# A streaming encoder step on one core: products of zeros and a small Exp ahead of the data, gate weights ahead of natural x, the norm's factor in two steps, gate tiles ahead of keys

## The chip, the cores and the metric

One NeuronCore of a Trainium2 chip. The metric is the device time in microseconds of one execution, lower is better. A core has TensorE (PE in the profile, with its weight loads as PEld), VectorE (DVE), ScalarE (ACT), GpSimd (POOL) and SyncE (SP, which here issues all transfers). Each engine works through its own list of instructions in order and waits on semaphores for the others.

## What is computed

One inference step of a two-layer encoder over 512 prompt frames and 8 streams of 16 sample frames, 640 rows of 1024 in all: a gated linear attention layer (GLA), a shared latent key and value side, and an attention layer that reads it. The change lies in the first layer:

```python
def gla_layer(x, S0, norm_pre, w_in, w_gate2, b_gate, head_norm, w_out, norm_post):
    h = rmsnorm(x, norm_pre)
    proj = h @ w_in
    q, k, v, gate, glr = jnp.split(
        proj, [KD_A, 2 * KD_A, 2 * KD_A + VD_A, 2 * KD_A + 2 * VD_A], axis=-1)
    z = (glr @ w_gate2 + b_gate).astype(jnp.float32)
    g = jax.nn.log_sigmoid(z) / GATE_TAU
    ...
    o, S = gla_core(heads(q, DK_A) * (DK_A ** -0.5), heads(k, DK_A), heads(v, DV_A),
                    heads(g, DK_A), S0.astype(jnp.float32))
    o = rmsnorm(o.transpose(0, 2, 1, 3), head_norm.reshape(H_A, DV_A)).reshape(B, T, VD_A)
    o = o.astype(x.dtype) * jax.nn.silu(gate)
    return x + rmsnorm(o @ w_out, norm_post), S
```

`gla_core` walks over chunks: scores of q times exp(b) and k times exp(-b), with b the running sum of g, times v, plus the carried state.

## The kernel before

All work is a list of steps that `steps()` (L115) writes out by hand; every engine runs through the list in order and does its part of each step, as `PARTS` says. A step's parts follow one another by semaphores (`after`). So the order in the list is the order in each engine's queue. Matrices are kept as a rounded part and a rest (hi, lo), so a product is three products on PE (`mm3`, L1477 to L1479).

The rows are 5 tiles of 128 (4 of the prompt, 1 of the samples). The first layer has 4 heads. Its steps near the change, in the order of the list:

- `xk k`: ACT scales a slice of transposed x (hat_hi, L949), DVE makes the rest (hat_lo, L1212). `piece name j`: a block of weights, loaded by SP into one of 4 stage buffers (`load_stage`, L736; the next load into a buffer waits until DVE has read it), rounded by ACT (slab_hi, L922), its rest by DVE (slab_lo, L1175). `vx k`: PE's products of slice k with v of head 0 and the low-rank gate, 5 tiles of 272 columns, 3 products each, 8 slices: 120.
- `xn t`: ACT sums the squares of natural x, tile t (L953). `rq`: POOL makes the norm's factor r and the products of it that others use (rr and so on, L861 to L866).
- `gf`, `gfh`, `gfl`: the low-rank gate times r, by DVE, ACT, DVE. `vg i`: v of head 0 times rr, by ACT and DVE, out of the banks of `vx` (three steps for five tiles). `glT`: PE transposes the low-rank gate (L1533), ACT copies it. `gw`: its second weight.
- `g0 t`: the output gate of head 0, tile t: 24 products, tanh on ACT (L970), product on DVE (L1229).
- `z u`: PE, then DVE (z_abs, L1235) and ACT (Exp, then `ln`: Ln, which loads another activation table, L979), `lg` and `lgh` (DVE, ACT, DVE), and then `c h`: PE's running sums (L1557).
- `qp h` and `k h`: query and key of head h, 48 products of 320 columns each; `em`, `e`, `q`, `qlo`, `klo`: the exponentials and their products. `kT`, `sc`, `U`, `os`, `Us`, `o`: transposed keys, scores, state update, and outputs of samples and prompt.

PSUM has 8 banks. Up to `c 3` they are given out by hand (`FIRST_BANKS`), then in a ring; a step on PE waits until the last reader of its banks is done (`before_bank`). `q_own`, `minus_half` and `gl3` are set by POOL before all else (L841 to L845).

Before, PE's order around the change is: vx 0 to 7, g0 0, glT, g0 1, z, qp 0, g0 2, c 0, k 0, c 1, kT 0, c 2, c 3, sc 0, U 0, g0 3, g0 4, os 0, Us 0, o 0, qp 1, k 1, v 1. SP's order is x and the first weights in turn, natural x (5 tiles), the two gate pieces of head 0, gate3, const, the gains, and then loads as buffers come free.

Of the kernel before, what the change touches and what calls it, by code (L numbers as in the profile page):

```python
# [28 lines left out]
VG = DV + RANK  # L29
Z_ORDER = (0, HA, 2, 3, 1)  # L30
# [84 lines left out]
def steps():  # L115
# [6 lines left out]
    for k in range(KD):  # L122
        out += [("xk", k)]
        if k % 2 == 0:
            out += [("piece", "v0g", k // 2)]
        out += [("vx", k)]
    out += [("xn", t) for t in range(NT)]
    out += [("rq",), ("const",), ("piece", ("g", 0), 0), ("gf",), ("piece", ("g", 0), 1), ("gfh",), ("gfl",), ("vg", 0), ("gw",)]
    out += [("g0", 0), ("glT",), ("vg", 1), ("vg", 2), ("piece", ("qk", 0), 0), ("g0", 1)]
    out += [("z", u) for u in Z_ORDER] + [("qp", 0), ("piece", ("qk", 0), 1)]  # L130
    out += [("ln", 0), ("lg", 0), ("ln", HA), ("lg", HA), ("ln", 2), ("lg", 2), ("lgh", 0), ("lgh", HA), ("ln", 3), ("lg", 3), ("ln", 1), ("lg", 1)]
    out += [("g0", 2), ("c", 0), ("em",), ("e", 0), ("lgh", 1), ("q", 0), ("lgh", 2), ("lgh", 3), ("qlo", 0), ("k", 0), ("klo", 0)]
    out += [("c", 1), ("kT", 0), ("c", 2), ("c", 3)]
    out += [("lds", 0)]
    for h in range(HA):
        last = h + 1 == HA
        if h:
            out += [("e", h), ("qp", h), ("q", h), ("k", h), ("qlo", h), ("klo", h)]
# [3 lines left out]
        if not h:  # L142
            out += [("vo",), ("U", h), ("g0", 3), ("sclo", h), ("g0", 4), ("Slo", h), ("stp", h)]
            out += [("piece", ("qk", 1), 0)]
# [10 lines left out]
        else:  # L155
            if not h:
                out += [("piece", ("qk", 1), 1), ("o", h)]
                load(("v", h + 1))
            else:
                load(("v", h + 1))  # L160
                out += [("o", h)]
            out += [("lds", h + 1)]
# [90 lines left out]
def samples(out, load):  # L253
# [26 lines left out]
    "och": ("sp",), "y0": ("pe", "act", "dve"), "oy": ("sp",), "keep": ("sp",), "ldk": ("sp",), "yt": ("pe", "act", "dve"), "sum": ("pool",), "xk": ("act", "dve"), "xn": ("act",), "vx": ("pe",), "rq": ("pool",), "gw": ("act", "dve"),  # L280
# [16 lines left out]
def parts(step):  # L297

    if step == ("c", 0):
        return ("pe",)  # L300
    if step[0] == "piece" and not any(w[5] for w in SLABS[step[1]][step[2]]):
        return ("sp", "act", "dve")
# [13 lines left out]
STAGED_NO = {s: n for n, s in enumerate(STAGED)}  # L316
FIRST_WEIGHTS = [STAGED_NO["piece", ("g", 0), j] for j in range(2)]
# [29 lines left out]
def read_out(step):  # L347

    if step[0] in ("qp", "z"):
# [10 lines left out]
FIRST_BANKS = {("vg", 0): (0, 1), ("vg", 1): (2, 3), ("vg", 2): (4,), ("g0", 0): (5,), ("glT",): (6, 7), ("g0", 1): (0,),  # L360
# [1468 lines left out]
```

## Time and profile before

| | us |
|---|---|
| three runs | 660.23, 659.3, 653.32 |
| median | 659.3 |
| the profiled execution | 654.99 |
| its span | 653.2 |
| PE busy in the span | 619.9 (95%) |
| DVE busy | 401.2 (61%) |
| ACT busy | 297.5 (46%) |
| mean granted TensorE clock | 0.991 |

PE is the engine that is busy nearly all the time; the others have room on average. Rows of the trace are read from the start of the span: the first number is the start in us, the second the length, and in brackets stands how long the engine sat idle before it and what ended that. A row with x5 groups five instructions in a row. TensorE's granted clock is given as a share of its full 2.4 GHz.

### The profile page before, as it was taken

The numbers are of one execution on the slowest core, as the hardware profiler recorded it, in microseconds if no ns is written. First come the engines' busy times: TensorE is split into PE (matmuls) and PEld (weight loads), VectorE is DVE, ScalarE is ACT, GpSimd is POOL, SyncE is SP. The second block draws the span as 40 slices with busy tenths as digits, with TensorE's granted clock in tenths as the row PEclk, the third lists the DMA queues.
The fourth block names the chain that finished last, engine by engine and source line by source line (L and its number), as shares of the span: only waits on it lengthen the run. The fifth ranks groups of instructions, "written<-read, shape, count | busy, mean of one in ns | idle before, by whom it ended". The sixth has DMA issues, their size and how long they took to land.

```text
span 653.2 us, 12063 instructions
## 1 busy us (share of the span) xinstructions
PE 619.9 (95%) x4702; PEld 598.4 (92%) x4702; DVE 401.2 (61%) x612; ACT 297.5 (46%) x578; POOL 123.7 (19%) x140
## 2 busy tenths in 40 slices
PE   5999999999999899997999999999999979989996
PEld 5989999999999799997999999988999978789996
DVE  5475755564564792258657767467788776664414
ACT  7785623432532352246323422365556667753311
POOL 0200200100030152236325400210000126630002
PEclk9999999999999899999999999999999999989999
DMA  8932280261262263232243410331111126766004
GB/s 317 332 108 65 64 259 18 66 204 55 74 193 66 73 228 112 83 112 98 67 113 84 129 65 2 112 85 30 34 29 38 49 81 199 236 214 255 1 1 162
DMA packets 66280, 73.68 MB, mean 113 GB/s; under 512 B 8112, under 2 KB 58544, under 8 KB 66096
## 3 DMA queue, kind: packets, MB, share of 16 engines
q1 hardware_dynamic: 66224, 72.91, 35.5%
q8 instruction: 38, 0.62, 0.4%
q14 instruction: 18, 0.15, 0.1%
HBM read 62.12 MB, written 10.78 MB: 112 GB/s over the span
## 4 chain that ended last, share of the span: by engine, by line
PE 64%; DVE 15%; ACT 11%; issue 4%; POOL 3%; DMA 3%; DVEq 0%; ACTq 0%; POOLq 0%
PE bank L1477 21%; PE bank L1479 20%; PE bank L1478 20%; DVE slab_lo L1175 2%; ACT prob L1109 2%; ACT slab_hi L922 2%; DVE pT_lo L1175 2%; DMA stage<-in_cache_ckv_dram 1%; DVE rows L1393 1%; DVE prob L1445 1%; DMA stage<-in_b_w_out_dram 1%; DVE qN_lo L1175 1%; DVE hat_lo L1175 1%; POOL skL L902 1%; POOL cn_lo L898 1%
## 5 line engine op out<-in xcount | busy, mean ns | idle before, releaser
L1477 PE MATMUL bank<-slab_hi,hat_hi 128*128 128x256 f32 (+2 forms) x600 | 171.8, 286 | 11.8 <-DVE slab_lo L1175 8.3
L1478 PE MATMUL bank<-slab_lo,hat_hi 128*128 128x256 f32 (+2 forms) x600 | 170.6, 284 | 0.0
L1479 PE MATMUL bank<-slab_hi,hat_lo 128*128 128x256 f32 (+2 forms) x600 | 170.5, 284 | 0.0
L1477 PEld LDWEIGHTS bank<-slab_hi,hat_hi 128*128 128x128 f32 x600 | 115.9, 193 | 12.7 <-DVE slab_lo L1175 8.5
L1478 PEld LDWEIGHTS bank<-slab_lo,hat_hi 128*128 128x128 f32 x600 | 116.0, 193 | 0.0
L1479 PEld LDWEIGHTS bank<-slab_hi,hat_lo 128*128 128x128 f32 x600 | 116.0, 193 | 0.0
L1175 DVE TENSOR_TENSOR slab_lo<-stage,slab_hi 128x1024 fp32r<-128x1024 f32 (+3 forms) x70 | 84.3, 1205 | 18.0 <-ACT slab_hi L922 16.0
L1477 PE MATMUL bank<-hat_hi,slab_hi 128*128 128x320 f32 x256 | 80.6, 315 | 0.6 <-DVE rows L1401 0.4
L1478 PE MATMUL bank<-hat_lo,slab_hi 128*128 128x320 f32 x256 | 79.8, 312 | 0.0
L1479 PE MATMUL bank<-hat_hi,slab_lo 128*128 128x320 f32 x256 | 79.7, 311 | 0.0
L922 ACT ACTIVATE slab_hi<-stage 128x1024 fp32r<-128x1024 f32 (+3 forms) x70 | 71.0, 1014 | 14.2 <-POOL stage L857 6.0
L1477 PEld LDWEIGHTS bank<-hat_hi,slab_hi 128*128 128x128 f32 x256 | 48.6, 190 | 1.4 <-DVE rows L1401 1.0
L1479 PEld LDWEIGHTS bank<-hat_hi,slab_lo 128*128 128x128 f32 x256 | 48.7, 190 | 0.0
L1478 PEld LDWEIGHTS bank<-hat_lo,slab_hi 128*128 128x128 f32 x256 | 48.7, 190 | 0.0
L1479 PE MATMUL bank<-slab_hi,oT_lo 128*128 128x256 f32 x160 | 45.4, 284 | 0.0
L1477 PE MATMUL bank<-slab_hi,qS 128*128 128x256 f32 x128 | 36.7, 287 | 0.0
L1478 PE MATMUL bank<-slab_lo,qS 128*128 128x256 f32 x128 | 36.3, 284 | 0.0
L876 POOL TENSOR_TENSOR stat<-stat,stat 128x1 f32<-128x1 f32 (+1 forms) x8 | 2.5, 311 | 169.6 <-ACT junk L1049 155.3
L1053 ACT ACTIVATE junk<-bank 128x256 bf16<-128x256 f32 x26 | 9.7, 384 | 51.1 <-PE bank L1479 51.1
L902 POOL TENSOR_TENSOR skL<-stage,skS 128x512 fp32r<-128x512 f32 x8 | 13.8, 1730 | 94.0 <-ACT skS L922 94.0
L1479 PEld LDWEIGHTS bank<-slab_hi,oT_lo 128*128 128x128 f32 x160 | 30.8, 193 | 0.0
L1171 DVE TENSOR_TENSOR y_rows<-bank,post 128x256 f32<-128x256 f32 (+1 forms) x14 | 7.5, 539 | 30.1 <-ACT junk L1053 19.6
(334 smaller groups left out, 1440.5 us busy)
## 6 DMA issues: line engine op xcount, KB each, us to landing
stage<-in_a_w_in_dram SPq DMA_DIRECT2D x22, 512.0 KB, 5.1
stage<-in_b_w_in_dram SPq DMA_DIRECT2D x10, 512.0 KB, 4.2
st_s<-in_state_gla_dram SPq DMA_DIRECT2D x4, 1024.0 KB, 7.0
out_dram<-st_s SPq DMA_DIRECT2D x4, 1024.0 KB, 5.3
stage<-in_a_w_out_dram SPq DMA_DIRECT2D x8, 512.0 KB, 4.6
stage<-in_ckvT_dram SPq DMA_DIRECT2D x8, 512.0 KB, 3.5
stage<-in_cache_ckv_dram SPq DMA_DIRECT2D x8, 512.0 KB, 4.1
stage<-in_b_w_out_dram SPq DMA_DIRECT2D x8, 512.0 KB, 3.9
```

What stands on the lines that cost most here:

```text
L898: last = pool.tensor_tensor(cn_lo[b][:, :, :], staged_as(kind, step), raw(cn_hi[b][:, :, :]), SUB)
L902: last = pool.tensor_tensor(skL[b][:, :], staged_as(kind, step), raw(skS[b][:, :]), SUB)
L922: return act.activation(out, in_, ACT.Copy)
L1053: last = act.activation(junk[:, i * 256:(i + 1) * 256], row[:, i * 256:(i + 1) * 256], ACT.Square, accum_out=S1(("y", ph, t), t=s))
L1109: last = act.activation(prob[u][:, c0:c0 + i + 1, :], bank[:, j, 0:(i + 1) * P].rearrange("p (s n) -> p s n", n=P), ACT.Exp, bias=S1(("S", ...
L1171: return dve.tensor_tensor(out, a, b, op)
L1175: return dve.tensor_tensor(lo, full, raw(hi), SUB)
L1393: last = dve.tensor_scalar(qln[:, t, :], qln[:, t, :], S1(("qa",), stat2, t), None, MUL)
L1445: last = dve.tensor_scalar(v, v, r[:, j:j + 1], None, MUL)
L1477: pe.matmul(out, a[0], b[0], start=first, stop=False)
L1478: pe.matmul(out, a[0], b[1], start=False, stop=False)
L1479: return pe.matmul(out, a[1], b[0], start=False, stop=last)
```

## The change

Six times PE multiplies q_own, all zeros, by itself as soon as it is set, ahead of everything else, into a bank that is written anew later; ACT takes an Exp of 8 columns of it. SP issues the two gate pieces of head 0 ahead of natural x, and const ahead of gate3; ACT and DVE take these pieces ahead of `xn`. `rq` ends with r; what is made from it is a step of its own, `rr`, and `vg` waits for that. On PE the order becomes: vx 0 to 7, g0 0, g0 1, glT, g0 2, z, qp 0, g0 3, c 0, g0 4, k 0, c 1, kT 0, c 2, c 3, sc 0, U 0, qp 1, os 0, Us 0, o 0, k 1, v 1, with other banks for it. The rest of the second piece of `qk 0` is taken from its step and becomes `plo`, behind the z products. The pieces of `qk 1` come earlier, and `qp 1` is copied by ACT into a part of the gate rows that is not yet in use, from where DVE takes it. The first weights of v 1 are taken ahead of `o 0`.

```diff
@@ -27,6 +27,7 @@
 VG = DV + RANK
+WARM = 6
 Z_ORDER = (0, HA, 2, 3, 1)
...
@@ -124,24 +125,24 @@
         out += [("vx", k)]
+    load(("g", 0))
     out += [("xn", t) for t in range(NT)]
-    out += [("rq",), ("const",), ("piece", ("g", 0), 0), ("gf",), ("piece", ("g", 0), 1), ("gfh",), ("gfl",), ("vg", 0), ("gw",)]
-    out += [("g0", 0), ("glT",), ("vg", 1), ("vg", 2), ("piece", ("qk", 0), 0), ("g0", 1)]
-    out += [("z", u) for u in Z_ORDER] + [("qp", 0), ("piece", ("qk", 0), 1)]
+    out += [("rq",), ("rr",), ("const",), ("gf",), ("gfh",), ("gfl",), ("vg", 0), ("g0", 0), ("gw",), ("g0", 1), ("glT",)]
+    out += [("vg", 1), ("vg", 2), ("piece", ("qk", 0), 0), ("g0", 2), ("piece", ("qk", 0), 1)]
+    out += [("z", u) for u in Z_ORDER] + [("qp", 0), ("plo", ("qk", 0), 1)]
...
-    out += [("g0", 2), ("c", 0), ("em",), ("e", 0), ("lgh", 1), ("q", 0), ("lgh", 2), ("lgh", 3), ("qlo", 0), ("k", 0), ("klo", 0)]
+    out += [("g0", 3), ("c", 0), ("em",), ("e", 0), ("lgh", 1), ("q", 0), ("g0", 4), ("lgh", 2), ("lgh", 3), ("qlo", 0), ("piece", ("qk", 1), 0), ("k", 0), ("klo", 0)]
     out += [("c", 1), ("kT", 0), ("c", 2), ("c", 3)]
...
         if h:
-            out += [("e", h), ("qp", h), ("q", h), ("k", h), ("qlo", h), ("klo", h)]
+            out += [("e", h)] + [("qp", h)] * (h > 1) + [("q", h), ("k", h), ("qlo", h), ("klo", h)]
             load(("g", h))
...
         if not h:
-            out += [("vo",), ("U", h), ("g0", 3), ("sclo", h), ("g0", 4), ("Slo", h), ("stp", h)]
-            out += [("piece", ("qk", 1), 0)]
+            out += [("vo",), ("U", h), ("qp", 1), ("sclo", h), ("Slo", h), ("stp", h), ("piece", ("qk", 1), 1)]
         else:
...
@@ -153,13 +154,8 @@
         else:
-            if not h:
-                out += [("piece", ("qk", 1), 1), ("o", h)]
-                load(("v", h + 1))
-            else:
-                load(("v", h + 1))
-                out += [("o", h)]
-            out += [("lds", h + 1)]
+            load(("v", h + 1))
+            out += [("o", h), ("lds", h + 1)]
     project_out(out, load, "A")
...
@@ -277,7 +273,7 @@
...
@@ -298,6 +294,10 @@
         return ("pe",)
+    if step == ("qp", 1):
+        return ("pe", "act")
+    if step == APART:
+        return ("sp", "act")
     if step[0] == "piece" and not any(w[5] for w in SLABS[step[1]][step[2]]):
...
@@ -314,6 +314,14 @@
 STAGED_NO = {s: n for n, s in enumerate(STAGED)}
+APART = "piece", ("qk", 0), 1
+
+
+def low_step(step):
+
+    return ("plo", *step[1:]) if step == APART else step
+
+
 FIRST_WEIGHTS = [STAGED_NO["piece", ("g", 0), j] for j in range(2)]
...
@@ -346,6 +354,8 @@
+    if step == ("qp", 1):
+        return "act", *step
     if step[0] in ("qp", "z"):
...
@@ -357,9 +367,9 @@
-FIRST_BANKS = {("vg", 0): (0, 1), ("vg", 1): (2, 3), ("vg", 2): (4,), ("g0", 0): (5,), ("glT",): (6, 7), ("g0", 1): (0,),
-               ("z", 0): (6,), ("z", HA): (7,), ("z", 1): (1,), ("z", 2): (2,), ("z", 3): (3,), ("qp", 0): (4, 5), ("g0", 2): (0,),
-               ("c", 0): (6, 7), ("k", 0): (2, 3), ("c", 1): (0, 1), ("kT", 0): (2, 3), ("c", 2): (6, 7), ("c", 3): (4, 5)}
+FIRST_BANKS = {("vg", 0): (0, 1), ("vg", 1): (2, 3), ("vg", 2): (4,), ("g0", 0): (5,), ("g0", 1): (6,), ("glT",): (0, 1), ("g0", 2): (7,),
+               ("z", 0): (0,), ("z", HA): (1,), ("z", 2): (2,), ("z", 3): (3,), ("z", 1): (6,), ("qp", 0): (4, 5), ("g0", 3): (7,),
+               ("c", 0): (0, 1), ("g0", 4): (6,), ("k", 0): (2, 3), ("c", 1): (6, 7), ("kT", 0): (2, 3), ("c", 2): (0, 1), ("c", 3): (4, 5)}
...
@@ -621,6 +631,8 @@
+        next_raw = rows[:, 3, D - TOK:D]
+
         def first_gate(t):
...
@@ -712,7 +724,7 @@
                     old = STAGED[n - NSTAGE]
-                    after(sp, parts(old)[-1], *old)
+                    after(sp, parts(old)[-1] if old != APART else "dve", *low_step(old))
                 if step[0] != "piece":
...
@@ -745,13 +757,13 @@
                     load_stage(k // 2)
+            for n in FIRST_WEIGHTS:
+                load_stage(n)
             for t in range(NT):
...
                              else dram["x_sample"].rearrange("b l d -> (b l) d")).then_inc(x_nat_in[t], 16)
-            for n in FIRST_WEIGHTS:
-                load_stage(n)
+            sp.dma_start(const[:, :], dram["const"]).then_inc(consts_in, 16)
             sp.dma_start(gate_raw[:, :], dram["gate3"]).then_inc(gate_in, 16)
-            sp.dma_start(const[:, :], dram["const"]).then_inc(consts_in, 16)
             for n, g in gain.items():
...
@@ -857,11 +869,13 @@
                     pool.wait_ge(done["act"], AT["act"][("xn", NT - 1)])
+                    r = S1(("r",), stat2)
+                    link(pool.tensor_scalar(r, S1(("x",)), 1.0 / D, EPS, MUL, ADD))
+                    last = pool.tensor_tensor(r, r, minus_half[:, 0:NT], ALU.pow)
+                elif kind == "rr":
                     r, rr = S1(("r",), stat2), S1(("rr",), stat2)
-                    link(pool.tensor_scalar(r, S1(("x",)), 1.0 / D, EPS, MUL, ADD))
-                    link(pool.tensor_tensor(r, r, minus_half[:, 0:NT], ALU.pow))
+                    link(pool.tensor_tensor(rr, r, r, MUL))
                     pool.tensor_scalar(S1(("rh",), stat2), r, 0.5, None, MUL)
-                    link(pool.tensor_tensor(rr, r, r, MUL))
                     pool.tensor_scalar(S1(("rrm",), stat2), rr, 1.0 / DV, None, MUL)
...
@@ -921,6 +935,8 @@
+            act.wait_ge(own_set, 1)
+            act.activation(junk[:, 0:8], q_own[:, 0, 0:8], ACT.Exp)
             act.wait_ge(first_gain_in, 16)
...
@@ -962,7 +978,7 @@
                 elif kind == "vg":
-                    act.wait_ge(done["pool"], AT["pool"][("rq",)])
+                    act.wait_ge(done["pool"], AT["pool"][("rr",)])
                     for t in range(2 * step[1], min(2 * step[1] + 2, NT)):
...
@@ -1007,6 +1023,8 @@
...
+                elif kind == "qp":
+                    last = copy(next_raw.rearrange("p (a n) -> p a n", a=2), bank[:, :, 0:HALF])
                 elif kind == "q":
...
@@ -1201,12 +1219,13 @@
                 bank, row = banks(step) if step in BANK_NO else (None, None)
-                if kind == "piece":
+                if kind in ("piece", "plo"):
                     _, name, j = step
+                    after(dve, "act", "piece", name, j)
                     m = used(name, j)
...
                     c = slice(j * PITCH[name], j * PITCH[name] + m)
-                    last = low(lo[:, c], stage[STAGED_NO[step] % NSTAGE][:, 0:m], hi[:, c])
+                    last = low(lo[:, c], stage[STAGED_NO["piece", name, j] % NSTAGE][:, 0:m], hi[:, c])
                 elif kind == "xk":
...
@@ -1247,8 +1266,12 @@
                         dve.wait_ge(own_set, 1)
-                    after(dve, "pe", "qp", h)
-                    v = banks(("qp", h))[0][:, :, 0:HALF]
+                    if h == 1:
+                        after(dve, "act", "qp", h)
+                        v = next_raw.rearrange("p (a n) -> p a n", a=2)
+                    else:
+                        after(dve, "pe", "qp", h)
+                        v = banks(("qp", h))[0][:, :, 0:HALF]
...
...
@@ -1506,6 +1529,9 @@
+            pe.wait_ge(own_set, 1)
+            for _i in range(WARM):
+                pe.matmul(pb[2][:, 1, 0:2 * P], q_own[:, 0:SB // 2, :], q_own[:, :, :].rearrange("p b n -> p (b n)"), start=True, stop=True)
             for step in STEPS:
...
@@ -1558,7 +1584,7 @@
                     h = step[1]
-                    after(pe, "dve", "piece", ("qk", h), 0 if kind == "qp" else 1)
+                    after(pe, "dve", *low_step(("piece", ("qk", h), 0 if kind == "qp" else 1)))
                     off = 0 if kind == "qp" else PIECE
...
                     for a in range(2):

```

## Rows read from the trace of the kernel before

**Rows 1.** The page's busy times and instructions by engine, whole span:
```profile
PE 619.9 (95%) x4702; PEld 598.4 (92%) x4702; DVE 401.2 (61%) x612; ACT 297.5 (46%) x578; POOL 123.7 (19%) x140
```

**Rows 2.** PE's waits, whole span: us in total, times, longest:
```profile
PE bank L1477 <- DVE slab_lo L1175: 8.3, 2, 7.9
...
PE bank L1557 <- DVE lg_lo L1175: 1.5, 1, 1.5
...
PE bank L1477 <- ACT decay L985: 0.4, 1, 0.4
```

**Rows 3.** Table by stretches: length, busy us (instructions), PEclk, DMA share, GB/s:
```profile
7.90:13.02 5.12, 5.12 (x23) 5.12 (x24) 4.93 (x6) 4.93 (x7) 0.00 (x0) 1.00 1.02 399
13.02:20.50 7.48, 7.48 (x61) 7.48 (x61) 3.41 (x5) 6.61 (x11) 0.00 (x0) 1.00 1.03 404
...
47.15:50.57 3.42, 3.42 (x16) 3.42 (x16) 0.73 (x3) 2.93 (x9) 0.00 (x0) 0.52 0.00 0
```

**Rows 4.** Timeline of PE in `k 0`: start, us, instruction:
```profile
47.34 0.47 PE L1478 MATMUL bank<-hat_lo,slab_hi 128*128 128x320 f32 x1
...
50.53 0.40 PE L1478 MATMUL bank<-hat_lo,slab_hi 128*128 128x320 f32 x1
...
55.60 0.31 PE L1479 MATMUL bank<-hat_hi,slab_lo 128*128 128x320 f32 x1
```

**Rows 5.** Timeline of ACT, start of the span:
```profile
3.86 1.28 ACT L949 ACT_TABLE_LOAD   x1 [3.86 <-DMA x_raw<-in_xT_dram]
...
6.02 0.66 ACT L922 ACTIVATE slab_hi<-stage 128x544 fp32r<-128x544 f32 x1
...
6.94 1.77 ACT L949 ACTIVATE hat_hi<-x_raw,gain_a_norm_pre 128x640 fp32r<-128x640 f32 x2 [0.26 <-DMA x_raw<-in_xT_dram]
```

**Rows 6.** Timeline of PE, the fp32 products of `os 0`:
```profile
69.43 1.07 PE L1614 MATMUL bank<-st_s,q_own 128*32 128x256 f32 x16
```

**Rows 7.** Timeline of ACT, POOL and DVE, the norm's factor:
```profile
20.50 1.06 ACT L953 ACTIVATE junk<-x_nat 128x1024 bf16<-128x1024 f32 x1 [0.19 <-DMA x_nat<-in_x_sample_dram]
...
23.51 1.06 ACT L922 ACTIVATE slab_hi<-stage 128x1024 fp32r<-128x1024 f32 x1 [0.45 <-DMA stage<-in_a_w_in_dram]
...
21.74 0.20 POOL L861 TENSOR_SCALAR stat<-stat 128x5 f32<-128x5 f32 x1 [19.78 <-ACT junk L953]
...
23.29 1.20 POOL L863 TENSOR_SCALAR stat<-stat 128x5 f32<-128x5 f32 x1
...
24.95 0.23 POOL L866 TENSOR_SCALAR stat<-stat 128x5 f32<-128x5 f32 x1
...
25.67 0.37 DVE L1171 TENSOR_TENSOR glf<-bank,stat 128x32 f32<-128x32 f32 x3 [1.28 <-PE bank L1479]
```

**Rows 8.** Timeline of ACT, DVE and PE, first v tiles and glT:
```profile
26.52 0.84 ACT L967 ACTIVATE vv_hi<-bank,stat 128x256 fp32r<-128x256 f32 x2
...
27.61 0.88 DVE L1226 SCALAR_TENSOR_TENSOR vv_lo<-bank,stat,vv_hi 128x256 fp32r<-128x256 f32 x2
...
28.88 0.71 PE L1533 MATMUL bank<-const,gl 128*128 128x128 f32 x5
```

**Rows 9.** Timeline of DVE, ACT and PE, from z to `c 0`:
```profile
34.68 3.59 DVE L1235 TENSOR_SCALAR z_abs<-bank 128x512 int32<-128x512 int32 x5
...
39.03 1.06 ACT L922 ACTIVATE slab_hi<-stage 128x1024 fp32r<-128x1024 f32 x1
...
40.11 1.28 ACT L979 ACT_TABLE_LOAD   x1
...
45.99 0.30 PE L1557 MATMUL bank<-const_r,lg_hi 128*128 128x130 f32 x1 [1.51 <-DVE lg_lo L1175]
```

**Rows 10.** Timeline of SP's DMA issues, DVE and POOL:
```profile
7.61 2.26 SPq L749 DMA_DIRECT2D x_nat<-in_x_prompt_dram  x4
...
9.73 0.72 DVE L1175 TENSOR_TENSOR slab_lo<-stage,slab_hi 128x544 fp32r<-128x544 f32 x1
...
31.53 2.48 POOL L869 TENSOR_SCALAR const_r<-const_raw 128x900 fp32r<-128x900 f32 x1 [6.35 <-DMA const_raw<-in_const_r_dram]
```

More of the change, by code:

```diff
@@ L279 @@
     "const": ("sp", "pool"), "piece": ("sp", "pool", "act", "dve"), "lds": ("sp",), "sts": ("sp",), "stp": ("sp",), "ldr": ("sp",),
-    "och": ("sp",), "y0": ("pe", "act", "dve"), "oy": ("sp",), "keep": ("sp",), "ldk": ("sp",), "yt": ("pe", "act", "dve"), "sum": ("pool",), "xk": ("act", "dve"), "xn": ("act",), "vx": ("pe",), "rq": ("pool",), "gw": ("act", "dve"),
+    "och": ("sp",), "y0": ("pe", "act", "dve"), "oy": ("sp",), "keep": ("sp",), "ldk": ("sp",), "yt": ("pe", "act", "dve"), "sum": ("pool",), "xk": ("act", "dve"), "xn": ("act",), "vx": ("pe",), "rq": ("pool",), "rr": ("pool",), "plo": ("dve",), "gw": ("act", "dve"),
     "gf": ("dve",), "gfh": ("act",), "vo": ("act",), "gfl": ("dve",), "vg": ("act", "dve"), "glT": ("pe", "act"), "g0": ("pe", "act", "dve"), "em": ("act",), "xT": ("pe", "act", "dve"),
```

## The prediction

> **What bounds the kernel now.** The page first: the products (PE) are busy 95% of the span [rows 1], so a change of order gains only where PE waits or runs slowly. The list of PE's waits, read next, shows three in the stretch that the diff touches: 8.3 us for slab_lo (7.9 of them before the first product, 0.4 more before the second half of the first gate tile), 1.5 for lg_lo, 0.4 for decay [rows 2]. The table by stretches shows what the waits leave out: between 7.90 and 13.02 us 23 products took 5.12 us (0.223 each), then 61 took 7.48 (0.123 each) [rows 3]. Same shape, twice the pace. The row's granted clock says 1.00 in both, so the record begins too late; 272 columns in 0.223 us is the 1.2 GHz level. At 47.15 to 50.57 the row itself says 0.52. It follows the 1.5 us wait. In `k 0` (48 products, the first at 47.13) the second starts at 47.34 and the fourteenth at 50.53, 0.266 apart; from there to the last the pace is (55.60-50.53)/34 = 0.149 [rows 4]. Lost: 12 x 0.117 = 1.4 us. So PE loses before 62 us: the late start, 23 x 0.100 = 2.3 slow, 0.4, 1.5, 1.4, 0.4. Behind 75 us the diff moves little, and a lead of PE there should reach the end.
>
> **Start: products of zeros, small Exp, and what they meet.** The table load runs 3.86 to 5.14, after x has landed; the first hat_hi follows it [rows 5]. The early Exp needs only a memset, so the load lies ahead of the data. The gain is not all of 1.28: the first slab_hi at 6.02 follows hat_hi at once, so the trace does not show when its weights had landed. Bounds 0 and 1.28; I take 0.6, the middle. The next hat_hi, 6.94, waits for DMA already, so no more than that is to be had.
>
> No row before shows full-width fp32 products. The nearest: 8 fp32 products of 32 by 256 columns (16 records) in 1.07 us [rows 6]. If four ran side by side, a full-width one costs 0.53; if not, 0.13. Six cost 0.8 to 3.2 us at full clock, twice that at half: they start near 1.2 and end between 2.8 and 7.6. Real work starts near 7.3, so they cost 0 to 0.3. Whether they raise the clock: before, it rose 5.1 us after the first product; six at the upper price are busy as long. I take it as up by about 7.3, the other bound being no effect. Then the 120 `vx` products take 120 x 0.123 = 14.8 and end at 22.1; without effect at 24.4. By the same rates they ended at 24.9 before (7.9 + 2.3 + 14.8).
>
> **The norm's factor decides what this is worth.** The gate weights (2 transfers) now go ahead of natural x (5). The seven move the same bytes, and the last of the seven was awaited by ACT until 23.51 before; the last x tile until 20.50 [rows 7]. So its square moves from 20.50 to about 23.4. From there, by rows of before: POOL starts 1.24 later (24.65), r is there 1.55 later (21.74 to 23.29: 26.2). `rr` must do the other four operations: they took 23.29 to 25.18, 1.9 us, of which one tensor_scalar is 1.20 while its like at 24.95 took 0.23. Bounds 0.9 and 1.9: rr at 27.1 to 28.1. `gf` and `gfl` no longer wait for rr (that is the split's gain, 0.9 to 1.9 on that branch). But the diff gives `glT` the banks (0, 1), which `vg 0` held, and these are free only when ACT and DVE have read v, for which they need rr: 0.84 + 0.88 and two handovers [rows 8], some 1.9. So `glT` can start at 29.0 to 30.0.
>
> PE gets there sooner: 22.1, then `g0 0` and `g0 1`, 24 products each (2.9), 27.9. It waits 1.1 to 2.1 us. Most of what the warm start gains is spent here; with no warm start it would arrive at 30.2 and hardly wait.
>
> The position "two gate tiles and glT done": before, 28.88 + 0.5 for the transposes (0.71 with their tail) + 2.9 = 32.3. After, 29.5 to 30.5. Ahead by 1.8 to 2.8.
>
> **Gate tiles ahead of keys.** `g0 2` moves ahead of the z products, `z` and `qp 0` are as before. Before, PE ran dry 1.51 us ahead of 45.99, at 44.48 [rows 9]; with the lead it gets there at 41.7 to 42.7, and `g0 3` (2.9) fills to 44.6 to 45.6. When are c 0's inputs ready? From glT's start DVE needed 5.8 us until its first z_abs (28.88 to 34.68); one more gate row is added and the row of g0 1 comes earlier, so I keep 5.8: 34.8 to 35.8. From z_abs to c 0 took 11.3; the weight piece's slab_hi (39.03, 1.06) leaves ACT's chain, and its slab_lo (`plo`) runs while ACT is still at Exp and the table load: 10.25. So c 0 at 45.05 to 46.05, beside 45.99 before, but with a fourth gate tile done. Ahead: 2.9 - 0.06 to 2.9 + 0.94, that is 2.8 to 3.8. What is late next is still this chain, by about half a microsecond.
>
> Two smaller moves on SP: const goes ahead of gate3 in the same group of transfers, and the load of const_r now stands behind two loads that wait for the gate pieces' slab_lo. POOL had const_r at 31.53 [rows 10] and c 0 needs it at 45; 3 or 4 us later costs nothing.
>
> With no long wait there, the slow stretch in `k 0` should go: 1.4. `g0 4` stands between c 0 and k 0 and only moves from later. Then c 1 takes banks (6, 7), so the scores no longer wait for ACT to empty c 2: 0.4. `qp 1` moves ahead of `os 0` and takes the place of g0 3 and 4; it is copied out by ACT (640 elements, so under the 1.06 of a piece with 1024 [rows 9]). Queued behind this copy on ACT are the second `qk 1` piece and the squares of os; for these POOL, then DVE wait, and `k 1` behind them. `qp 1` no longer lies between os and k 1, so 48 x 0.149 = 7.2 us less cover; what is left are Us and `o 0`, and behind them `k 1` (7.2) and `v 1` (96 products, 11.8) for the state update on DVE. I cost this at nothing; if the cover fails, it is the copy and the piece, up to 2.1.
>
> **The sum.** 2.8 to 3.8, plus 1.4, plus 0.4: 4.6 to 5.6, middle 5.1. The profiled execution took 655.0 us (span 653.2 and 1.8 around it): 649.9. But the three runs are 653.3, 659.3 and 660.2; the median is 4.3 above the profiled one. I know no reason for the changed kernel to fall on the quick side, so I take the middle of 655.0 and 659.3, 657.1, and predict 652.0.
>
> **Rivals.**
> 1. *The factor comes in time* (0.14). x lands sooner or POOL and the v tiles are quicker, and glT does not hold PE: 1.1 to 2.1 more, gain near 7, 650. For: rr's price rests on one odd row. Against: seven transfers came back to back, and ACT waited for them.
> 2. *The clock falls in the new wait* (0.24). The wait at glT is 1.1 to 2.1 us, and a wait of 1.5 came ahead of the slow stretch before [rows 2, 3]. Price 1.4, perhaps again in z and the c 0 chain: gain 3.0 to 3.7, 654. Against: the products on both sides of it are dense, while before c 0's small ones followed. The Trainium skill (TensorE: Matmul & The Clock Gate, section HAM oscillation — how this bites in real kernels) says that gaps between bursts of products bring the clock down again and that each burst then starts slow; by it the new gap speaks against this change. The trace agrees in that the slow stretch stands behind a wait; by the rule the sum is 651.3 on the profiled execution.
> 3. *Nothing net* (0.08). The z chain starts 3 us later than I put it (more queued on DVE between v and the gate rows), c 0 with it, and its wait is back with the slow stretch: 657.
> 4. *Slower* (0.04). SP issues natural x behind the second gate piece, and that waits for DVE to have emptied the second stage buffer, 10.45 before (9.73 + 0.72) [rows 10]. If the transfers ahead ran dry meanwhile, x would be late, and each microsecond goes one for one into the factor, glT, z and c 0. It decides from 5 us on (x at 28.5); over 1% slower needs 12, 668. Against: x used to be issued from 7.61 on, and what was queued by then kept the queue full far beyond 10.45.
>
> **How the numbers follow.** The forecast has 0.50. About 1% (6.6 us) is what a measurement of this kernel can tell from no change. Against the median of 659.3 the forecast is 7.3 below, so it counts as faster about as often as two times in three (0.33 to 0.17 same); rival 1 is faster (0.12 of 0.14), rival 2 less often (0.07 of 0.24); what is left of these and rival 3 are same (0.17 + 0.02 + 0.17 + 0.08 = 0.44, of which 0.01 goes to slower for the spread of the runs); rival 4 is slower. Faster 0.52, same 0.43, slower 0.05. Range: from rival 1 at the quick runs (653.3 - 7 = 646) to rival 3's 657 and a little: 646 to 657.5.
>
> **What would show it.** The first vx product before 7.9 and a pace of 0.123 there at once (or 0.223: no effect). The last x tile's square at 23 to 24 and the glT transposes at 29 to 30, behind a wait of PE for DVE's v tiles. No wait over 1 us ahead of c 0, no 1.2 GHz stretch in k 0, scores without their wait on decay. k 1 over some 5 us sooner than before. A second slow stretch at 28 to 34 says rival 2; glT near 28 without a wait says rival 1; a slab_lo or st_s wait ahead of k 1 or v 1 would be a cost I put at nothing.

## The result and the profile after

| | before | changed |
|---|---|---|
| median (18 runs of each) | 655.07 us | 650.69 us |
| lowest to highest | 651.35 to 660.3 | 647.64 to 654.42 |
| ratio, 95% interval | | 0.9945 [0.9924, 0.9965] |
| profiled execution (its span) | 654.99 (653.2) | 652.62 (650.8) |
| mean granted clock in it | 0.991 | 0.988 |

The changed kernel is 4.4 us faster between the medians. The ratio puts the gain at 0.55% (0.35 to 0.76%, or 2.3 to 5.0 us): clear of zero, but less than the 1% that the prediction called faster.

Busy times of the page of the changed kernel, the first number being PE's, and PE's waits up to 105 us (us in total, times, longest). They answer to [rows 1, 2].

```profile
PE 623.5 (96%) x4714; PEld 600.6 (92%) x4714; DVE 401.2 (62%) x612; ACT 298.4 (46%) x580; POOL 123.8 (19%) x140
...
PE bank L1559 <- DVE vv_lo L1245: 2.3, 1, 2.3
PE bank L1500 <- DVE slab_lo L1193: 1.5, 2, 1.3
PE bank L1534 <- POOL q_own L853: 1.1, 1, 1.1
PE bank L1601 <- DVE kt L1189: 0.8, 1, 0.8
```

PE is busy for 3.6 us more than before [rows 1]; the products of zeros add 4.4. Of the 8.3 for slab_lo 1.5 is left, beside 1.1 ahead of the zeros; the 1.5 for lg_lo and the 0.4 for decay [rows 2] are gone; a wait of 2.3 for the v tiles (vv_lo) and one of 0.8 for kt are new.

PE's timeline of the changed kernel: the zeros, the first vx products, glT with the gate tile behind it, z, c 0, the first and last of k 0, kT 0, kT 1.

```profile
1.08 4.41 PE L1534 MATMUL bank<-q_own 128*128 128x256 f32 x12 [1.08 <-POOL q_own L853]
6.81 0.36 PE L1500 MATMUL bank<-slab_hi,hat_hi 128*128 128x272 f32 x1 [1.32 <-DVE slab_lo L1193]
7.01 0.29 PE L1501 MATMUL bank<-slab_lo,hat_hi 128*128 128x272 f32 x1
7.14 0.29 PE L1502 MATMUL bank<-slab_hi,hat_lo 128*128 128x272 f32 x1
...
30.53 0.76 PE L1559 MATMUL bank<-const,gl 128*128 128x128 f32 x5 [2.28 <-DVE vv_lo L1245]
31.05 0.36 PE L1500 MATMUL bank<-slab_hi,hat_hi 128*128 128x256 f32 x1
35.50 0.56 PE L1569 MATMUL bank<-gate,glT 128*128 128x128 f32 x4
...
47.43 0.22 PE L1583 MATMUL bank<-const_r,lg_hi 128*128 128x130 f32 x1
...
51.42 0.31 PE L1500 MATMUL bank<-hat_hi,slab_hi 128*128 128x320 f32 x1
58.31 0.31 PE L1502 MATMUL bank<-hat_hi,slab_lo 128*128 128x320 f32 x1
...
60.47 0.74 PE L1601 MATMUL bank<-const,kt 128*128 128x128 f32 x5 [0.78 <-DVE kt L1189]
...
97.43 0.71 PE L1601 MATMUL bank<-const,kt 128*128 128x128 f32 x5
```

The second vx pair is 0.13 apart at once, where before 23 products took 0.223 each [rows 3]. The last row is kT 1, the first step behind v 1; up to there both kernels have done the same real products in another order. Before, it stood here:

```profile
100.49 0.71 PE L1575 MATMUL bank<-const,kt 128*128 128x128 f32 x5
```

So the lead is 3.1 us in these two executions. From kT 1 to the end of the span it is 552.7 before and 553.4 after.

Table by stretches of the changed kernel: length, PE busy and its instructions, the other engines, then PEclk, DMA share, GB/s.

```profile
6.81:22.30 15.49, 15.30 (x120) 15.12 (x121) 10.82 (x12) 12.22 (x17) 0.00 (x0) 1.00 1.03 384
...
31.60:35.00 3.40, 3.40 (x18) 3.40 (x17) 2.13 (x6) 2.87 (x5) 0.06 (x1) 0.50 0.42 140
...
51.42:58.31 6.89, 6.89 (x49) 6.89 (x48) 4.51 (x9) 3.96 (x6) 0.00 (x0) 1.00 0.00 0
```

All 120 vx products run at the full clock; k 0 has no slow stretch any more (0.147 a product throughout, against [rows 3, 4]). A slow one, at 1.2 GHz, stands behind the new wait instead: gate tile 2 takes 35.50 - 31.05 = 4.45 us where 24 products at full clock take 2.9.

The norm's factor in the changed kernel, from the timelines of ACT, POOL and DVE (answering to [rows 5, 7, 8]):

```profile
0.72 1.28 ACT L939 ACT_TABLE_LOAD   x1 [0.72 <-PEq L1827]
...
5.16 0.66 ACT L936 ACTIVATE slab_hi<-stage 128x544 fp32r<-128x544 f32 x1 [0.46 <-DMA stage<-in_v0g_dram]
...
24.85 1.06 ACT L969 ACTIVATE junk<-x_nat 128x1024 bf16<-128x1024 f32 x1 [0.15 <-DMA x_nat<-in_x_sample_dram]
...
28.66 0.84 ACT L983 ACTIVATE vv_hi<-bank,stat 128x256 fp32r<-128x256 f32 x2 [0.20 <-POOL stat L880]
...
26.09 0.20 POOL L873 TENSOR_SCALAR stat<-stat 128x5 f32<-128x5 f32 x1 [24.12 <-ACT junk L969]
26.37 1.18 POOL L874 TENSOR_TENSOR stat<-stat,minus_half 128x5 f32<-128x5 f32 x1
27.63 0.20 POOL L877 TENSOR_TENSOR stat<-stat 128x5 f32<-128x5 f32 x1
27.92 0.25 POOL L878 TENSOR_SCALAR stat<-stat 128x5 f32<-128x5 f32 x1
...
27.64 0.37 DVE L1189 TENSOR_TENSOR glf<-bank,stat 128x32 f32<-128x32 f32 x3 [7.47 <-POOL stat L874]
28.56 0.24 DVE L1193 TENSOR_TENSOR gl<-glf,gl 128x80 fp32r<-128x80 f32 x1 [0.55 <-ACT gl L936]
29.60 0.88 DVE L1245 SCALAR_TENSOR_TENSOR vv_lo<-bank,stat,vv_hi 128x256 fp32r<-128x256 f32 x2 [0.79 <-ACT vv_hi L983]
```

One chain ends in glT's wait: the last x tile lands, its square starts at 24.85, r is ready at 27.6, rr at 28.6, ACT makes v's rounded part, DVE its rest until 30.48, and glT starts at 30.53. Its own operand, the low-rank gate gl, is done at 28.80: the last 1.7 us of the wait are for banks 0 and 1, which hold v's first tiles until then and which the change gave to glT. No run gives it other banks, so what that would bring is open.

### The profile page after: what moved, and what is told of

Its sections match the earlier page's. It is cut to its first block, busy times and chain, and to the rows that moved or that the text cites. A ratio compares the mean times of both kernels' runs of the same rounds, so it can differ in the third digit from the quotient of the medians.

```text
span 650.8 us, 12087 instructions
## 1 busy us (share of the span) xinstructions
PE 623.5 (96%) x4714; PEld 600.6 (92%) x4714; DVE 401.2 (62%) x612; ACT 298.4 (46%) x580; POOL 123.8 (19%) x140
## 4 chain that ended last, share of the span: by engine, by line
PE 62%; DVE 16%; ACT 10%; DMA 4%; issue 4%; POOL 3%; SPq 1%; DVEq 0%; ACTq 0%; POOLq 0%
PE bank L1500 20%; PE bank L1502 19%; PE bank L1501 19%; DVE slab_lo L1193 2%; ACT prob L1127 2%; DMA x_nat<-in_x_sample_dram 2%; DVE pT_lo L1193 2%; DMA stage<-in_cache_ckv_dram 2%; ACT slab_hi L936 1%; DVE rows L1189 1%; DVE rows L1416 1%; DMA stage<-in_v0g_dram 1%; DVE prob L1468 1%; DVE qN_lo L1193 1%; POOL skL L916 1%
## 5 line engine op out<-in xcount | busy, mean ns | idle before, releaser
L1127 ACT ACTIVATE prob<-bank,stat 128x512 f32<-128x512 f32 (+3 forms) x32 | 16.6, 524 | 19.6 <-DVE stat L1458 19.4
```

What stands on the lines that cost most here:

```text
L1127: last = act.activation(prob[u][:, c0:c0 + i + 1, :], bank[:, j, 0:(i + 1) * P].rearrange("p (s n) -> p s n", n=P), ACT.Exp, bias=S1(("S", ...
```

## The experiments

Theory T: the norm's factor, held by the landing of natural x, sets when v's tiles leave their banks and so when glT starts; all that brings PE to glT sooner becomes waiting there, and from glT on the order with gate tiles ahead of keys keeps PE fed. A part of T, written into the expectations, was that the zeros even cost time, as the longer wait lets the clock fall. Rivals are named with each run. "kT 1" is the place in PE's timeline just used: 100.49 before, 97.43 in the changed kernel. Times are medians in us; the kernel before had 654.1 to 655.3 beside them.

**Without the zeros, and without zeros and Exp.**

```diff
-WARM = 6
+WARM = 0
```

> The changed kernel without its six products of zeros (the early Exp stays). Theory T: the products of glT wait for v's tiles and so for the norm's factor, at about 30.5 us, whenever PE gets there; the lead of the warm start is spent in that wait (2.3 us), and the clock falls behind it. Without the zeros vx runs at the 1.2 GHz level for some 5 us, ends near 24.6 instead of 22.3, the second gate tile near 30.4, glT starts at 30.5 after a wait under 0.4, no 1.2 GHz stretch follows, and kT 1 (97.4 in the changed kernel, 100.5 before) starts at 96.0. Time 1 to 2 us under the changed kernel's 650.7. Rival R: the warm start is what the change gains; without it all is 2.3 us later: kT 1 at 99.7, time 653.

648.15 in 4 runs, ratio 0.9891 [0.9857, 0.9926]. glT of this kernel, and the stretch behind it:

```profile
30.49 0.76 PE L1559 MATMUL bank<-const,gl 128*128 128x128 f32 x5 [0.19 <-DVE vv_lo L1245]
```

```profile
31.60:35.00 3.40, 3.40 (x31) 3.36 (x30) 2.12 (x6) 3.27 (x6) 0.13 (x1) 1.00 0.36 125
```

vx ends 2.0 later (24.3), and glT starts at the same place, 30.5, with next to no wait: what the zeros gain is waited away in full. kT 1 is at 96.41.

In the second kernel the small Exp on ACT is left out as well:

```diff
-            act.wait_ge(own_set, 1)
-            act.activation(junk[:, 0:8], q_own[:, 0, 0:8], ACT.Exp)
```

> The changed kernel without the zeros and without the early Exp. T: the first weights are rounded at 6.0 instead of 5.2, so 0.9 more than without the zeros alone; the second gate tile ends near 31.2, glT follows without a wait, no 1.2 GHz stretch behind it, kT 1 near 96.7. R: 3.2 us later than the changed kernel: kT 1 at 100.6.

651.55 (one run); kT 1 at 96.75.

```profile
30.27 0.71 PE L1557 MATMUL bank<-const,gl 128*128 128x128 f32 x5
```

With neither zeros nor Exp the new order alone has 100.49 - 96.75 = 3.7 us of the lead. The Exp adds 0.3, but not at glT: it starts here without a wait, and in the three profiles with the Exp and no zeros at 29.95, 30.49 and 30.50. The 0.3 arises behind glT: DVE's slab_lo at 34.38 took 1.86 us, as POOL's const_r had started 0.16 ahead of it, and 1.23 in the run without zeros, where it started first. So no part of the new start is seen to make glT earlier.

**The start alone, in the order of before.** The Exp and six products of zeros put into the kernel before, nothing else:

```diff
+            act.wait_ge(own_set, 1)
+            act.activation(junk[:, 0:8], q_own[:, 0, 0:8], ACT.Exp)
...
+            pe.wait_ge(own_set, 1)
+            for _i in range(6):
+                pe.matmul(pb[2][:, 1, 0:2 * P], q_own[:, 0:SB // 2, :], ...)
```

> The kernel before with only the new start: the early Exp and the six products of zeros. T: vx starts at 6.8 and ends at 22.3 (25.2 before), but the first gate weights are still rounded by 24.4 and 25.9, so g0 0 waits about 2 us and glT comes at 28.4 instead of 28.9; all later waits stay, so kT 1 is 0.5 sooner than the 100.5 of before, and if the clock falls in the new wait ahead of g0 0 it is about 1 later. Time within 1 us of the kernel before. R (the warm start is the gain): 3 us sooner, kT 1 at 97.5.

658.72 in 10 runs, ratio 1.0049 [1.0006, 1.0093]: no gain, rather a loss; kT 1 at 100.83. PE's waits in this kernel show where the early start went, and the stretch has its clock:

```profile
25.18 0.38 PE L1479 MATMUL bank<-slab_hi,hat_hi 128*128 128x256 f32 x1 [2.54 <-DVE slab_lo L1177]
27.68 0.39 PE L1479 MATMUL bank<-slab_hi,hat_hi 128*128 128x256 f32 x1 [0.81 <-DVE slab_lo L1177]
```

```profile
25.20:28.00 2.80, 1.99 (x14) 1.78 (x15) 1.90 (x6) 1.51 (x5) 0.62 (x4) 1.00 1.15 308
```

The first gate tile waits for its weights, 3.3 us in all. They were also taken later than before, the second piece at 24.20 in place of 23.51 [rows 7], and glT came at 29.23, 0.35 after the 28.88 of before [rows 8]: that is the loss at kT 1. The clock did not fall behind the wait of 2.5.

**Zeros ahead of glT as well.** Five more of the same products, just ahead of the step glT:

```diff
+                if kind == "glT":
+                    for _i in range(5):
+                        pe.matmul(pb[3][:, 1, 0:2 * P], q_own[:, 0:SB // 2, :], ...)
```

> The changed kernel with five more products of zeros on PE ahead of glT, into a bank that is not in use, to fill its wait. T: glT still at 30.5, but the clock does not fall behind it: the third gate tile takes 2.9 us instead of 4.3, kT 1 at 96.0 instead of 97.4, time 649.2. R (the stretch at 1.2 GHz has nothing to do with that wait, or products of zeros do not hold the clock): the stretch at 31 to 35 stays, kT 1 at 97.4, 650.7.

649.88 in 4 runs, ratio 0.9909 [0.9874, 0.9945].

```profile
27.89 2.32 PE L1541 MATMUL bank<-q_own 128*128 128x256 f32 x10
30.19 0.77 PE L1562 MATMUL bank<-const,gl 128*128 128x128 f32 x5
```

The wait is filled, the clock stays up, kT 1 comes at 96.10, as expected. Against the changed kernel's profile that is 1.3, mostly the slow stretch of that execution; against its second profile (96.32, at the end of this section), in which the clock stayed up without these zeros, it is 0.2. So it is not shown that the zeros held the clock.

**Natural x made early.** Only one tile of x is loaded and squared five times; four tiles' factors are therefore the first one's, and 2 MB less are moved.

```diff
-            for t in range(NT):
-                sp.dma_start(x_nat[:, t, :], ...).then_inc(x_nat_in[t], 16)
+            sp.dma_start(x_nat[:, 0, :], dram["x_prompt"][0, 0:P, :]).then_inc(x_nat_in[0], 16)
...
-                    act.wait_ge(x_nat_in[t], 16)
-                    last = act.activation(junk[:, :], x_nat[:, t, :], ...)
+                    act.wait_ge(x_nat_in[0], 16)
+                    last = act.activation(junk[:, :], x_nat[:, 0, :], ...)
```

> The changed kernel with one tile of natural x loaded instead of five, squared five times, so that the factors of four tiles are those of the first; 2 MB less is transferred. T: the factor is there by 25, glT starts when PE gets to it, near 28.1, no wait over 0.3 and no 1.2 GHz stretch at 31; qp 0 near 34, c 0 near 44.5, kT 1 at 93.5 to 94.5, 3 to 4 us sooner than the changed kernel. R (glT's wait is not for the factor): as the changed kernel, 97.4.

646.49 (2 runs), ratio 0.9862 [0.9765, 0.9959]; kT 1 at 94.54.

```profile
28.61 0.76 PE L1557 MATMUL bank<-const,gl 128*128 128x128 f32 x5 [0.62 <-DVE vv_lo L1243]
...
44.73 0.30 PE L1581 MATMUL bank<-const_r,lg_hi 128*128 128x130 f32 x1 [0.42 <-DVE lg_lo L1191]
```

The changed kernel's second profile, which has no slow stretch here either, has the last square at 24.69, glT at 30.38, c 0 at 46.49 and kT 1 at 96.32. Here they come at 22.93, 28.61, 44.73 and 94.54: all 1.8 sooner. What delays the squares goes one for one into glT, c 0 and kT 1. This is T's main step, shown by taking its cause away. glT came 0.5 later than expected, because ACT's five squares, back to back from 18.19 on, now hold the factor.

**Natural x ahead of the gate weights again**, on SP and in the order of ACT and DVE, the rest of the change kept:

```diff
-    load(("g", 0))
     out += [("xn", t) for t in range(NT)]
+    load(("g", 0))
...
-            for n in FIRST_WEIGHTS:
-                load_stage(n)
             for t in range(NT):
...
+            for n in FIRST_WEIGHTS:
+                load_stage(n)
```

> The changed kernel with natural x ahead of the gate weights again, in SP's list and in ACT's. T: the same bytes must have landed, so the factor is early (r near 23.4) but the gate weights are rounded by 24.4 and 25.9; vx ends at 22.3, g0 0 waits 2 us there, runs to 27.2 or so, g0 1 to 30.1, glT follows at 30.2 without a wait. The wait has only moved from glT to g0 0: kT 1 within 0.5 us of the changed kernel if the clock falls there too, 1.4 sooner if not. R (the order of the loads is what brings the gain): kT 1 2 us or more later than 97.4.

654.29 in 10 runs, ratio 0.9965 [0.9921, 1.001]; kT 1 at 99.78. The wait moves to the first gate tile and is longer than expected:

```profile
25.84 0.58 PE L1500 MATMUL bank<-slab_hi,hat_hi 128*128 128x256 f32 x1 [3.65 <-DVE slab_lo L1193]
```

```profile
24.10:30.90 6.80, 5.06 (x23) 5.06 (x24) 3.94 (x8) 2.56 (x5) 3.23 (x5) 0.50 1.16 290
```

The expected wait was 2 us: T missed its size, 3.7, and the two gate tiles then ran at 1.2 GHz. The gate weights were the late ones now: DVE had the two pieces ready at 25.8 and 27.2, where T had put 24.4 and 25.9. At kT 1 this is 2.4 us behind the profile of the changed kernel (3.5 behind its second one), which is the mark of R (2 or more) and not T's (0.5): loading the gate weights first is worth that much, though it delays x.

**The factor in one step again** (rq and rr merged, everything that used r waits for rr):

```diff
-    out += [("rq",), ("rr",), ("const",), ("gf",), ...
+    out += [("rq",), ("const",), ("gf",), ...
...
-                    act.wait_ge(done["pool"], AT["pool"][("rr",)])
+                    act.wait_ge(done["pool"], AT["pool"][("rq",)])
```

> The changed kernel with the norm's factor made in one step again. T: gf waits for the four later operations too (0.9 us), and vg 0, which follows it on ACT, with it: glT at 31.2 to 31.4, kT 1 0.7 to 0.9 later than 97.4. R (vg 0 waits for the products of r anyway, so the split is worth nothing): unchanged.

649.79 (one run); kT 1 at 98.16.

```profile
31.21 1.33 PE L1557 MATMUL bank<-const,gl 128*128 128x128 f32 x5 [1.91 <-DVE vv_lo L1243]
```

glT starts 0.7 later than in the changed kernel although x was 0.2 earlier: the two steps are worth some 0.9 us at glT, by one profile of each. In this execution the clock fell behind the wait, as in the changed kernel's.

**Gate tiles one place earlier each**: g0 2 ahead of glT, g0 3 ahead of z, g0 4 ahead of c 0, so none is left between c 0 and k 0.

```diff
-    out += [..., ("g0", 1), ("glT",)]
-    out += [..., ("piece", ("qk", 0), 0), ("g0", 2), ("piece", ("qk", 0), 1)]
+    out += [..., ("g0", 1), ("g0", 2), ("glT",)]
+    out += [..., ("piece", ("qk", 0), 0), ("g0", 3), ("piece", ("qk", 0), 1)]
...
-    out += [("g0", 3), ("c", 0), ("em",), ("e", 0), ("lgh", 1), ("q", 0), ("g0", 4), ("lgh", 2), ...
+    out += [("g0", 4), ("c", 0), ("em",), ("e", 0), ("lgh", 1), ("q", 0), ("lgh", 2), ...
```

> The changed kernel with each gate tile one place earlier on PE: the third ahead of glT, the fourth ahead of z, the fifth ahead of c 0, and none between c 0 and k 0. T: the third tile fills the wait; glT at 31.0 without one, the fourth covers ACT's copy of glT and the key weights, z at 34.4, qp 0 at 36.3, c 0 at 46.6 with all five tiles done, no 1.2 GHz stretch; kT 1 3.0 to 3.6 us sooner than 97.4, near 94; time 647. R: the tiles only change places, no work goes away: kT 1 at 97.4, 650.7.

A miss: 656.72 in 12 runs, ratio 1.0021 [0.9996, 1.0045], kT 1 at 103.46 instead of 94. glT's wait went, as expected (0.2 is left). But the tiles needed other banks as well (FIRST_BANKS, not shown above): g0 3 now holds bank 5, for which qp 0 waits 1.1 us at 37.6, and a slow stretch follows. And then, on PE and in the table by stretches:

```profile
61.67 1.06 PE L1601 MATMUL bank<-const,kt 128*128 128x128 f32 x5 [3.16 <-DVE kt L1189]
```

```profile
38.00:41.40 3.40, 3.40 (x15) 3.40 (x15) 3.23 (x6) 2.69 (x5) 0.00 (x0) 0.51 0.53 157
61.90:72.10 10.20, 10.20 (x50) 10.20 (x49) 2.54 (x4) 4.73 (x16) 0.00 (x0) 0.50 0.67 217
```

The tile between c 0 and k 0 had been cover for the chain from c 0 to kt (table load, exponentials, q's and k's products). Without it PE waits 3.2 at kT 0 and then runs 10.2 us at half the clock, by estimate a loss of 5.1 on top. The missing tile is not all of it, as the kernel before has none there either and did not wait: 1.2 of the 3.2 are DVE's slab_lo of the first qk 1 piece, which runs from 59.45 to 60.67, right ahead of kt, and which the change had moved there.

**Gate tile 3 behind c 0**, on the kernel without zeros:

```diff
-    out += [("g0", 3), ("c", 0), ("em",), ("e", 0), ...
+    out += [("c", 0), ("g0", 3), ("em",), ("e", 0), ...
```

> The changed kernel without its products of zeros (as in the run without zeros, which had c 0 at 46.60 after a wait of 0.4 and kT 1 at 96.41), and with gate tile 3 moved from ahead of c 0 to behind it. T (gate tiles ahead of c 0 are cover: without them TensorE stands still until c 0's operands come, and its clock falls behind the gap): TensorE idle ahead of c 0 about 3.4 us in place of 0.4, the granted clock at its lower level behind it, kT 1 at 100.3 to 100.8, and the whole some 4 us longer than without this move. Rival (the tile only changes its place, as the products are the same): kT 1 at 96.4 to 97 and no change of the time.

663.73 (2 runs), ratio 1.0139 [1.0095, 1.0183], kT 1 at 108.91: the direction was right, the size was not. PE, the table by stretches and ACT of this kernel:

```profile
46.06 0.44 PE L1583 MATMUL bank<-const_r,lg_hi 128*128 128x130 f32 x1 [3.29 <-DVE lg_lo L1193]
```

```profile
46.10:51.70 5.60, 5.60 (x26) 5.60 (x27) 1.12 (x2) 0.00 (x0) 0.00 (x0) 0.50 0.00 0
...
65.40:79.10 13.70, 13.36 (x61) 13.39 (x62) 4.54 (x9) 6.57 (x19) 0.00 (x0) 0.50 0.52 163
```

```profile
52.95 1.28 ACT L986 ACT_TABLE_LOAD   x1 [6.88 <-PE bank L1502]
54.24 0.47 ACT L986 ACTIVATE rows<-bank,stat 128x256 f32<-128x256 f32 x1
54.75 0.77 ACT L1019 ACTIVATE Em<-bank 128x384 f32<-128x384 f32 x2
```

The wait of 3.3 ahead of c 0 and the slow clock behind it came as expected. What the expectation lacked is ACT: the list is its queue too, so Em now stands behind the tanh of gate tile 3, ACT idles 6.9 us for that tile, and Em comes at 54.75 instead of 48.47 in the kernel without zeros. kT 0 is late by a second wait, of 1.9, with 13.7 us at 1.2 GHz behind it.

**Zeros or none, side by side.** The first comparison had the kernel without zeros 2.5 us below the changed one, but from different sets of runs. Both were therefore timed together.

> The changed kernel without its products of zeros, timed side by side with the changed kernel on one chip. T (the zeros bring TensorE to the wait at glT earlier, which does not make the wait's end earlier, and the clock falls behind it): 1 to 2.5 us below the changed kernel, about 0.990 of the kernel before where the changed kernel has 0.9945. Rival (the difference seen so far is the spread of the runs): the same time as the changed kernel within 0.5 us.

> The changed kernel unaltered, as the reference point for the kernel without zeros: about 0.9945 of the kernel before, 650.7 us; a wait of some 2.3 us at glT with the granted clock at its lower level behind it, and kT 1 at about 97.4. T: 1 to 2.5 us above the kernel without zeros on the same chip. Rival: the same as that kernel within 0.5 us.

Without zeros 649.78 (12 runs, 646.37 to 652.92), ratio 0.9934 [0.9909, 0.996]; changed 650.04 (6 runs, 648.36 to 651.75), ratio 0.9932 [0.9905, 0.9959]. This part of T fell: the difference left, 0.3, is far inside the spread of the runs. The changed kernel's second profile shows why:

```profile
30.38 0.77 PE L1559 MATMUL bank<-const,gl 128*128 128x128 f32 x5 [2.02 <-DVE vv_lo L1245]
...
96.32 0.71 PE L1601 MATMUL bank<-const,kt 128*128 128x128 f32 x5
```

```profile
31.60:35.00 3.40, 3.40 (x31) 3.36 (x30) 2.16 (x5) 3.24 (x7) 0.10 (x1) 1.00 0.41 138
```

The same wait of 2 us, and the clock stayed up behind it. kT 1 is at 96.32, beside 96.44 without zeros. The slow stretch behind glT belonged to that one execution of the changed kernel, not to every one. At glT (30.38, 30.50 without zeros) and at kT 1 the zeros gain next to nothing; in the time, 12 and 6 runs leave room for some 1.5 us either way. No version measured here that reads all of x is surely quicker than the changed kernel.

## Why the prediction was right, and where it was not

**The total: 652.0 against 650.7**, for two errors that offset in part, so that the number came this close is luck. The gain was put at 5.1 and is 4.4 between the medians (4.2 at kT 1 without the slow stretch, 3.1 with it). The base was put at 657.1, halfway between the profiled execution and the median of three runs; with 18 runs the median of before is 655.07, the profiled execution's own time. The range, 646 to 657.5, would have held a gain of nothing as well. The same base misled the chances: the larger one, 0.52, went to faster by over 1%, because the forecast was counted against 659.3. It came out within 1% (0.43).

**Start.** Right in kind and size: first vx product 1.1 sooner (7.90 to 6.81; 0.6 taken within 0 to 1.28), full pace at once, end at 22.3 (22.1). At the start a product of zeros takes 4.41/6 = 0.73 us, inside the bounds of 0.13 to 1.06 with the half clock counted. It cost nothing because PE then idled 1.32 anyhow. (A slip that bears on nothing: 7.9 + 2.3 + 14.8, the end of vx before, is 25.0 and not 24.9; the trace has 25.4.)

**The factor.** The place was right, the arithmetic behind it nearly so. The square was put at 23.4 and came at 24.85, behind a wait of 0.15 for its tile. The seven transfers did come back to back, but the last of them was late, whatever their order: with natural x first again it was taken at 24.80 too. The rate does not explain it. From 7.9 to 20.5 us the changed kernel moved 386 GB/s against 402 before, but the run without zeros and Exp moved 387, and its last square started at 23.86 without a wait. The lateness goes with the early Exp: the ten profiles that have it and load all of x took the last of the seven at 24.2 to 25.2, the two that don't at 23.51 and 23.86. Two are few, and why it should be so is not settled.

rr came at its lower bound, 0.9. The odd 1.20 [rows 7] was no property of the operation but a wait: before, it ran from 23.29 to 24.49, beside DVE's work on a gate piece:

```profile
23.16 1.23 DVE L1175 TENSOR_TENSOR slab_lo<-stage,slab_hi 128x1024 fp32r<-128x1024 f32 x1 [6.59 <-ACT slab_hi L922]
```

The change takes that piece out of the way, and the same tensor_scalar takes 0.25. Where natural x goes first again, two of rr's operations start 0.15 and 0.17 behind such a slab_lo and take 1.13 and 1.14.

Together glT starts at 30.4 to 30.5, beyond 29.0 to 30.0. The sentence that without a warm start PE "would arrive at 30.2 and hardly wait" is what the run without zeros shows (30.1, wait 0.2); in its second profile vx was at full pace sooner, and PE came at 29.4 and waited 1.0.

**The z chain and c 0.** From glT to c 0 the prediction had 5.8 + 10.25 = 16.05; the second profile has 46.49 - 30.38 = 16.1. So c 0's lateness against 45.05 to 46.05 is all glT's, and of the gain of 5.1 about 0.9 (30.4 against the middle of 29.5) was lost to this one mis-sized term: the landing of x.

**Rival 2 happened in one profile of two.** A slow stretch at 31.6 to 35.0, price 1.5 by gate tile 2's 4.45 (1.4 had been put). The rule of the Trainium skill named with it (TensorE: Matmul & The Clock Gate, section HAM oscillation — how this bites in real kernels) says that gaps between bursts bring the clock down. The traces agree in part: behind gaps of 1.51 (before, [rows 9]), 2.28 (changed), 1.91 (one step), 3.65 (x first), 3.29 (gate tile 3 behind c 0), 1.09 and 3.16 (gate tiles early) it fell, behind 2.02 (changed again) and 2.54 (the start alone) it did not. In these rows the gap's length does not decide it.

**Costs put at nothing.** qp 1 ahead of os 0 and const_r later: no wait of PE over 0.8 stands between c 0 and kT 1 in the changed kernel, so that was right. The pieces of qk 1 were not free. DVE now makes the first one's rest in the middle of `k 0`, from the timeline of the changed kernel:

```profile
58.24 1.22 DVE L1193 TENSOR_TENSOR slab_lo<-stage,slab_hi 128x1024 fp32r<-128x1024 f32 x1
59.50 0.82 DVE L1189 TENSOR_TENSOR kt<-bank,Em 128x640 f32<-128x640 f32 x1
```

PE had finished `k 0` by 58.6, and kt comes 0.9 later; PE waits 0.78 for it at kT 0 (0.37 in the second profile). Without this slab_lo kt would be done, by estimate, at 59.5, when PE is still at c 1 (to 59.7). No run leaves it out. The wait on decay is gone as said. Rival 4 (x late by 5 us or more) did not come; x was late by 1.4 against the forecast.

**Which part did it.** The order (gate tiles, loads, banks) alone has 3.7 of the lead at kT 1; the small Exp has 0.3, by a chance of timing between DVE and POOL, and the zeros 0.1, by one profile of each. The prediction had said that most of the warm start is spent at glT; it is all spent there.

## What to carry to other kernels

Before paying for an earlier start, find the next fixed point on the path, here glT behind the norm's factor, and ask when its inputs land and its banks come free: what is gained ahead of it is waiting time unless they come earlier too. Independent work is worth most where a long chain of the other engines ends (the gate tiles around c 0), and moving one such tile by one place cost 14 us: PE stood still twice and ran at 1.2 GHz behind each stop, and a list that all engines follow moved ACT's queue along with PE's. Take a base from more than three runs before counting chances of 1%.

## What was not expected of the hardware

The runs of one kernel spread over 7 to 9 us, and the granted clock goes with it: among the changed kernel's 18, 0.998 came with 647.75 us, 0.988 with 652.62 and 0.986 with 654.42. In the profiles the difference lies in good part in stretches of some 3.4 us at 1.2 GHz in code that the change doesn't touch. They stand near the same places, but not at each of them in every execution: in the changed kernel's profile at 219, 308 and 533 us, in its second one at 217 (6.8 long) and 531, without zeros at 217 alone and in the second profile at 218, 307 and 532. Where PE is busy, each costs by estimate some 1.7 us (half of 3.4), more than several of the parts of this change are worth.

DVE and POOL held each other up where DVE's slab_lo (two operands out of SBUF) and a POOL operation overlapped. A POOL operation of 0.2 us that started just behind a slab_lo took 1.1 to 1.2 and ended 0.05 to 0.1 us after it (before, the start alone, x first). The slab_lo itself, 1.23 us, took 1.86 and 1.64 where POOL's const_r had started 0.16 (without zeros and Exp) and 0.37 (gate tiles early) ahead of it.
